# GpSimd subtracts the rests of 18 weight units in a two-layer trunk with routed experts

## What is computed

```python
def reference(x, ...):
    for l in range(2):
        h = rms_norm(x, g_attn_norm[l])
        x = x + merged_attention(h) @ w_out[l]          # two attention branches, gated
        h = rms_norm(x, g_ffn_norm[l])
        if l % 2 == 0:
            x = x + swiglu(h, dense_w_gate[0], dense_w_up[0], dense_w_down[0])
        else:
            x = x + moe_swiglu(h, w_router[0], moe_w_gate[0], moe_w_up[0], moe_w_down[0])
    return rms_norm(x, g_final)

def swiglu(h, w_gate, w_up, w_down):
    return (silu(h @ w_gate) * (h @ w_up)) @ w_down     # moe: top 2 of 8 experts, 1024 -> 3584 -> 1024
```

## Time and profile before

| | |
|---|---|
| runs before | 1463.18, 1461.19, 1462.83 us; median 1462.83 |
| profiled execution | 1463.33 us, its span 1461.5 us |
| granted TensorE clock, mean | 0.997 of full speed |
| busy: TensorE / VectorE / ScalarE / GpSimd | 1415.6 / 1198.6 / 1014.9 / 52.4 us |
| weight loads in the expert stage | 336 of 1 MB, 9.4 to 9.6 us from issue to landing |
| HBM read | 447.85 MB |

### The profile page before, as it was taken

How to read it: one execution, slowest core, us unless ns; L and a number is a source line. 1 busy time by engine, 2 the same in 40 slices (tenths; PEclk the granted TensorE clock), 3 DMA queues, 4 the chain that set the end, 5 groups by cost and what they waited for, 6 DMA issues and landing times.

```text
span 1461.5 us, 17502 instructions
## 1 busy us (share of the span) xinstructions
PE 1415.6 (97%) x6728; PEld 1152.5 (79%) x6728; DVE 1198.6 (82%) x1062; ACT 1014.9 (69%) x1003; POOL 52.4 (4%) x61
## 2 busy tenths in 40 slices
PE   9999999999999999999889999889999899999997
PEld 7877888888887788887668887668887667888885
DVE  5777655556678769989998889999889999889896
ACT  6566544335565677778887778887778887777774
POOL 1000000000000028000000000000000000001000
PEclk9999999999999999999999999999999999999999
DMA  9934555545653449999999999999999999999992
GB/s 350 365 102 138 180 201 195 179 143 192 191 180 123 154 162 407 421 372 404 421 421 418 381 366 396 421 422 414 400 377 377 419 422 422 417 370 367 420 387 94
DMA packets 96488, 460.06 MB, mean 315 GB/s; under 512 B 7656, under 2 KB 13304, under 8 KB 53392
## 3 DMA queue, kind: packets, MB, share of 16 engines
q1 hardware_dynamic: 91632, 444.63, 78.7%
q10 hardware_dynamic: 3312, 9.46, 1.8%
q0 software_dynamic: 1456, 4.79, 0.8%
HBM read 447.85 MB, written 11.01 MB: 314 GB/s over the span
## 4 chain that ended last, share of the span: by engine, by line
PE 70%; DVE 13%; DMA 10%; ACT 4%; issue 2%; SPq 0%; ACTq 0%; DVEq 0%
PE A L446 15%; PE A L448 15%; PE A L447 15%; DMA raw<-in_moe_w_down 9%; DVE wlo L421 7%; PE DN L446 5%; PE DN L448 5%; PE DN L447 5%; DVE wlo_more L421 2%; ACT whi L414 2%; PE T L1955 1%; DMA xs<-in_x 1%; PE A L1675 1%; PE T L448 1%; PE T L447 1%
## 5 line engine op out<-in xcount | busy, mean ns | idle before, releaser
L421 DVE TENSOR_TENSOR wlo<-raw,whi 128x2048 fp32r<-128x2048 f32 (+2 forms) x335 | 752.8, 2259 | 136.7 <-ACT whi L414 135.0
L414 ACT ACTIVATE whi<-raw 128x2048 fp32r<-128x2048 f32 (+2 forms) x335 | 632.4, 1894 | 207.7 <-PE A L448 91.2
L421 DVE TENSOR_TENSOR wlo_more<-raw,whi_more 128x2048 fp32r<-128x2048 f32 x84 | 192.1, 2286 | 23.1 <-ACT whi_more L414 22.9
L414 ACT ACTIVATE whi_more<-raw 128x2048 fp32r<-128x2048 f32 x84 | 161.1, 1918 | 35.3 <-PE A L448 14.2
L446 PE MATMUL A<-whi,hTh 128*128 128x512 f32 (+2 forms) x448 | 174.4, 389 | 1.7 <-DVE wlo L984 0.9
L447 PE MATMUL A<-wlo,hTh 128*128 128x512 f32 (+2 forms) x448 | 169.9, 379 | 0.0
L448 PE MATMUL A<-whi,hTl 128*128 128x512 f32 (+2 forms) x448 | 169.8, 379 | 0.0
L446 PE MATMUL A<-whi,heTh 128*128 128x512 f32 x420 | 166.5, 396 | 0.0
L448 PE MATMUL A<-whi,heTl 128*128 128x512 f32 x420 | 163.9, 390 | 0.0
L447 PE MATMUL A<-wlo,heTh 128*128 128x512 f32 x420 | 163.6, 389 | 0.0
L452 PE MATMUL A<-whi,heTh 128*128 128x512 f32 x252 | 107.2, 425 | 8.1 <-DVE wlo L421 7.8
(11 more groups left out here) (359 smaller groups left out, 2083.8 us busy)
## 6 DMA issues: line engine op xcount, KB each, us to landing
raw<-in_moe_w_gate SPq DMA_DIRECT2D x112, 1024.0 KB, 9.4
raw<-in_moe_w_up SPq DMA_DIRECT2D x112, 1024.0 KB, 9.6
raw<-in_moe_w_down SPq DMA_DIRECT2D x112, 1024.0 KB, 9.6
raw<-in_w_in SPq DMA_DIRECT2D x22, 1024.0 KB, 6.5
raw<-in_dense_w_down SPq DMA_DIRECT2D x11, 1024.0 KB, 4.9
raw<-in_dense_w_gate SPq DMA_DIRECT2D x10, 1024.0 KB, 5.1
raw<-in_dense_w_up SPq DMA_DIRECT2D x10, 1024.0 KB, 5.1
raw<-in_w_out SPq DMA_DIRECT2D x8, 1024.0 KB, 5.0
```

The costliest lines, as they stand in the source:

```text
L414: nc.scalar.activation(split_slot(u, e)[0][:, :n], raw[:, u % R, :n], ACT.Copy).then_inc(hi_done, 1)
L421: nc.vector.tensor_tensor(lo[:, :n], raw[:, u % R, :n], hi[:, :n].bitcast(F32), ALU.subtract).then_inc(lo_done, 1)
```

## The change

Of each small expert's 42 units, six have their rest subtracted by GpSimd: in groups 1 to 6 the fourth unit, the second up unit, numbers 7, 13, 19, 25, 31 and 37. `POOLED` lists them, counted through the experts: 18 in all. GpSimd does them after its work on the rows and before it waits for the gathers; each waits for `hi_done` and adds one to a semaphore of its own, `pool_lo`. VectorE leaves them out, and `lo_done` counts the others; `rests_before` is the number of rests on `lo_done` ahead of a unit. TensorE and SyncE wait through `rest_there`, on the one semaphore or the other.

```diff
--- before.py
+++ after.py
@@ -91,6 +91,9 @@
 
 SMALL = P // 2
 SMALL_AT = (1, 3, 5)
+
+
+POOLED = [e * EU + group_at(j) + 3 for e in SMALL_AT for j in range(1, EG)]
 
 
 G_LAYER = KD + KQ + KKV + KD
@@ -370,6 +373,7 @@
         pool_own = sem("pool_own")
 
         ordered = sem("ordered")
+        pool_lo = sem("pool_lo")
         gate_out, folded, low_out = sem("gate_out"), sem("folded"), sem("low_out")
         oe_full, oe_act, oe_dve = sem("oe_full"), sem("oe_act"), sem("oe_dve")
         last_full, last_added, last_squared = sem("last_full"), sem("last_added"), sem("last_squared")
@@ -394,6 +398,16 @@
 
         def in_main(u):
             return UM <= u < UM + NE * EU
+
+        def is_pooled(u, e=None):
+            return u < UM + NE * EU and u + times(e, EU) - UM in POOLED
+
+        def rests_before(u, e=None):
+
+            if u >= UM + NE * EU:
+                return u - len(POOLED) + times(e, EU)
+            u += times(e, EU)
+            return u - sum(g < u - UM for g in POOLED)
 
         def split_slot(u, e=None):
 
@@ -415,11 +429,20 @@
 
         def split_lo(dve, u, e=None):
 
+            if is_pooled(u, e):
+                return
             n = UNIT if u >= UM else units[u][1] * units[u][2]
             dve.wait_ge(hi_done, u + 1 + times(e, EU))
             hi, lo = split_slot(u, e)
             nc.vector.tensor_tensor(lo[:, :n], raw[:, u % R, :n], hi[:, :n].bitcast(F32), ALU.subtract
                                     ).then_inc(lo_done, 1)
+
+        def rest_there(eng, u, e=None):
+
+            if is_pooled(u, e):
+                eng.wait_ge(pool_lo, POOLED.index(u + times(e, EU) - UM) + 1)
+            else:
+                eng.wait_ge(lo_done, rests_before(u, e) + 1)
 
         class Lead:
 
@@ -514,8 +537,10 @@
                 sp.dma_start(xT[:, c], x_turned[:, c]).then_inc(turned_landed[i], 16)
 
             def load(u, dst_u, src, kt, n, e=None):
-                if u >= R:
-                    sp.wait_ge(lo_done, u - R + 1 + times(e, EU))
+                if u >= UM + NE * EU:
+                    sp.wait_ge(lo_done, u - R + 1 - len(POOLED) + times(e, EU))
+                elif u >= R:
+                    rest_there(sp, u - R, e)
                 sp.dma_start(raw[:, dst_u, :kt * n].rearrange("p (k n) -> p k n", k=kt), src
                              ).then_inc(raw_landed[dst_u], 16)
 
@@ -1922,7 +1947,7 @@
                 few = is_small(n, e)
 
                 def products(u, h, bank, border=False):
-                    pe.wait_ge(lo_done, u + 1 + e * EU)
+                    rest_there(pe, u, e)
                     for kk in range(4):
                         k = 4 * h + kk
                         if border:
@@ -1992,7 +2017,7 @@
                         pe.wait_ge(ff_lo[1], EG * n + j + e * EG)
                         ud = base + down_at(j - 1, EG)
                         for i in range(2):
-                            pe.wait_ge(lo_done, ud + i + 1 + e * EU)
+                            rest_there(pe, ud + i, e)
                             for kk in range(2):
                                 k = 2 * i + kk
                                 for h in range(2):
@@ -2103,6 +2128,10 @@
                 done(pool.tensor_copy(slot_out[:, r, :], row_sum[:]))
                 of_turn(r, kept_comb, back_w[:, r, :])
             pool.sem_inc(weights_known, 1)
+            for g in POOLED:
+                pool.wait_ge(hi_done, UM + g + 1)
+                hi, lo = split_slot(UM + g)
+                pool.tensor_tensor(lo, raw[:, (UM + g) % R, :], hi.bitcast(F32), ALU.subtract).then_inc(pool_lo, 1)
             pool.wait_ge(scattered, 16 * 2 * NB)
             pool.wait_ge(rows_landed_out, 16 * (NE - 1))
             for b in range(NB):

```

## The result

| | before | with the change |
|---|---|---|
| median | 1463.01 us (4 runs, 1461.19 to 1464.0) | 1499.01 us (4 runs, 1494.68 to 1503.61) |
| ratio | | 1.0247, 95% interval 1.0228 to 1.0266 |
| profiled execution, span | 1461.5 us | 1501.8 us |
| granted TensorE clock, mean | 0.997 | 0.988 |

The change costs 36 us; 1490 was forecast, in a range of 1467 to 1510. The profiled execution is the slowest of its four, 40.3 us above that of before, and its details have to be read with that in mind.

A forecast was written before the change was run, and what follows sets the result against it. VectorE and the loads, nearly level, were taken to bound the small experts. With GpSimd and VectorE as one queue, 98.9 - 90.0 = 8.9 us per expert, three times 26.7, on 1463.3 gave 1490 us; range 1467 to 1510.

The forecast's parts named there:

- The bound: In small experts (104 us), VectorE and the load stream, nearly level, set the pace; TensorE does not.
- the rests are the pace for the first third: In each small expert VectorE's subtractions set the pace for the first third, the loads for the remainder.
- side-by-side rival: GpSimd and VectorE run together, loads alone pace small experts: at most 2.5 us won each, 1455 to 1457; chance 0.14.
- Exclusion: GpSimd and VectorE subtractions of SBUF tensors lock each other out, assumed symmetrical, forming one queue; full exclusion 0.67.
- half exclusion: GpSimd runs while VectorE is idle or reads PSUM: +3.0 us per small expert, +9, 1472 us; chance 0.10.
- The price: One GpSimd subtraction of 128x2048 takes 4.3 us (range 4.0 to 4.6), plus 0.2 for two handovers.
- The sum: Per small expert 66.0 + 27.0 + 5.9 = 98.9 us against 90.0: 8.9 more, 26.7 for three; 16.4 per group.
- the mark: In each small expert, from VectorE's `oe` copy to its sixth `aTh`: mean 90.0 us, forecast to grow to about 99.
- nothing is added: In the small experts' queues, `av`'s wait for TensorE's use of the moved unit is covered by VectorE's earlier work.
- The clock: Idler TensorE in small experts runs partly at 1.2 GHz: 1555 us, mild case 1508; clock or longer chains 0.09.
- The signs: 18 fewer VectorE subtractions, GpSimd's 4.3 to 6.5 us, mark about 99, loads near 380 GB/s, `whi` not waiting for `raw`.

The follow-up runs named there:

- tiny kernel: Changed kernel with GpSimd subtracting only the first 16 of 2048 columns of its 18 units, all waits kept: 1465.02 us, ratio 1.0001 against the kernel before.
- the copy: Changed kernel with GpSimd copying the raw unit into the rest in place of subtracting, 18 units: 1463.44 us, ratio 0.9989 against the kernel before.
- the down unit moved: Changed kernel with GpSimd given each group's second down unit in place of its second up unit, same dose: 1485.57 us, ratio 1.0144.
- order-and-clock kernel: Changed kernel with GpSimd also waiting for VectorE's units ahead of its own, plus ten idle TensorE products before up products in groups 1 to 6: 1484.81 us, ratio 1.0152.
- run with idle products: Changed kernel with ten idle TensorE products ahead of the up products of groups 1 to 6 in each small expert: 1490.44 us, ratio 1.0175.

## Why the prediction was right, and where it fell short

**The bound.** VectorE near its limit and the loads level with it: right. But "the rests are the pace for the first third" was taken as time to be won, 2.5 us per expert in the side-by-side rival. The tiny kernel won nothing. The rate of 412 GB/s against 422 was no sign of loads held back by VectorE. By my reading, in the stretch that VectorE filled first the loads had run ahead, and what it had gained there it would have waited for later; that wasn't tried by itself.

**Exclusion.** Read from GpSimd's small operations that waited for VectorE, and taken to hold the other way: shown, by the trio of 11.05 us and by the copy in both directions. The side-by-side rival falls. Of half exclusion so much is true that `aTh` and `av` run beside GpSimd where the order lets them: with the down unit moved a group took 16.0 us, not 16.3.

**The price.** Estimated at 4.3 us and 0.2 for the handovers, from the step between 128x2 and 128x16; VectorE stood 4.37 us, and the undisturbed record is 4.58. The 4497 ns that the Trainium skill (GPSIMD Engine Reference, section 3.1) gives for an addition lies between the two. The step from the smallest instructions to one 128 times as long held to 3% in what VectorE stood, and to 6% in the length of the record.

**The sum.** 16.4 us per group: 16.3 in ten of the 15 groups of the changed kernel, 16.3 with order and clock mended. This part of the 36 us was sized nearly rightly: the order-and-clock kernel costs 22.3 us over its own before (1484.8 to 1462.5), and 26.7 had been forecast. Of the 4.4 between them 18 x 0.13 = 2.3 are the hold of 4.37 for 4.5; the rest is by my estimate slack behind the sixth `aTh`, which the mark left out: 106.8 - 90.0 = 16.8 us stand there against 16.2 of VectorE's work, 0.6 per expert.

**What failed** is the sentence on the queues: "nothing is added". It followed the moved unit (its `av`, its load, its slot) and found all of that covered. It did not follow the unit that was overtaken. The prediction even states the race, with unit 14: "GpSimd takes 13 when its `whi` is there; VectorE then meets 14 first and stands." In 11 of the 18 cases it was so. In the other seven the one that stood was the unit before, 12 here, since the `whi` of the moved unit was there before VectorE had begun it; and 12 carries fold, silu and ScalarE's queue. Each time that cost 2.3 to 3.0 us, 18.4 in the profiled execution, and by the run with idle products some two thirds of it was TensorE's clock. **The clock** had been a rival of its own, by idler groups in general; what the trace shows is narrower, a wait of 3.7 us and 3.6 to 5.7 us at the lower clock behind it. Order and clock together are 14.2 us by the combined run (or more, by what the idle products cost there); less the 4.4 that is 9.8, and 9.3 lie between 26.7 and 36.0. That the forecast of 1490 came within 9 us owes something to luck too: the sum was 4.4 too high where the queues were put at nothing.

**The signs.** The 18 fewer subtractions and GpSimd's 6.3 us where it met one running came as forecast; the loads fell to 369 GB/s, below the 380. The mark grew to 101.7 us, not 99, and `whi` did not wholly stop waiting for `raw`: ScalarE waited 3.6 us for it from 659 to 765 us, 14.7 before.

## What to carry to other kernels

Before an operation is moved to GpSimd, ask whether it reads SBUF while VectorE works on two SBUF tensors: then the two engines are one queue, and a subtraction that takes 2.20 us of it on VectorE takes 4.37 on GpSimd. The cost is a threshold, set by what else paces the stage: the same 18 units cost 36 us where the loads left 0.75 us per group, and under 3 where TensorE left 2.4, or 3 where the dose was halved. An engine that may take its work as soon as it is ready can overtake a unit that is needed sooner, so after the moved step follow also the one that it can overtake.

## What the runs showed of the hardware that I had not expected

GpSimd's copy of 128x2048 float32 takes 1.90 us and its memset 1.81, against 4.58 for the subtraction: two inputs cost more than double of one, and the copy is quicker than VectorE's 2.20 for a subtraction. The memset ran at full speed in all 18 cases, five of them inside a two-input operation of VectorE. And behind a TensorE wait of 3.7 us the products came at nearly half the rate, 0.43 us apart: from the first on at 759.29, and only after 1.1 us at 689.07.
